# Strassen's seven products for the first feed-forward layer of a two-block decoder kernel, with its results kept in DRAM

## What is computed

```python
h = _rms(x, norm2_w[l]) * (1 + sc2) + sh2
x = x + g2 * (jnp.square(jax.nn.relu(h @ w_ff1[l])) @ w_ff2[l])
```

## Time and profile before

| | |
|---|---|
| median of three runs | 3284.92 us (3284.49 to 3287.08) |
| profiled execution: its own time | 3284.06 us |
| profiled execution: span, first to last instruction | 3282.3 us |
| PE busy | 3189.7 us, 97% |
| DVE, ACT, POOL busy | 45%, 26%, 35% |
| granted TensorE clock, mean | 0.993 |

### The profile page before, as it was taken

How to read it: one execution, slowest core, us unless ns; L and a number is a source line. 1 busy time by engine, 2 the same in 40 slices (tenths; PEclk the granted TensorE clock), 3 DMA queues, 4 the chain that set the end, 5 groups by cost and what they waited for, 6 DMA issues and landing times.

```text
span 3282.3 us, 39103 instructions
## 1 busy us (share of the span) xinstructions
PE 3189.7 (97%) x15278; PEld 2618.6 (80%) x15278; DVE 1463.8 (45%) x2213; ACT 863.1 (26%) x1410; POOL 1152.1 (35%) x880
## 2 busy tenths in 40 slices
PE   8999999998999899999999999999999999999999
PEld 5778888887787676788888888788788878888887
DVE  6765666566345775642222333336214731313131
ACT  4454445444222231400232233201101310101010
POOL 2332121221366321233222222353335753434342
PEclk9999999999999999999999999999999999999999
DMA  3321011100243221155123122421113321111112
GB/s 136 102 74 39 26 33 33 33 26 26 78 145 118 71 84 39 53 173 170 45 61 79 54 76 72 129 65 52 45 52 126 93 74 49 51 46 52 45 52 78
DMA packets 92208, 234.21 MB, mean 71 GB/s; under 512 B 7680, under 2 KB 33920, under 8 KB 91920
## 3 DMA queue, kind: packets, MB, share of 16 engines
q1 hardware_dynamic: 53504, 186.67, 18.4%
q10 hardware_dynamic: 38544, 45.24, 4.5%
HBM read 212.84 MB, written 19.04 MB: 71 GB/s over the span
## 4 chain that ended last, share of the span: by engine, by line
PE 91%; DVE 6%; ACT 2%; issue 1%; DMA 1%; ACTq 0%; SPq 0%; DVEq 0%
PE proj_bank L229 24%; PE proj_bank L231 23%; PE proj_bank L230 23%; PE aux_banks L229 3%; PE aux_banks L230 3%; PE aux_banks L231 3%; PE aux_banks L781 2%; PE aux_banks L862 2%; PE aux_banks L788 1%; PE aux_banks L1797 1%; PE aux_banks L2277 1%; PE aux_banks L563 1%; DVE aux_banks L1675 1%; PE aux_banks L2298 1%; DVE dil_k L2445 0%
## 5 line engine op out<-in xcount | busy, mean ns | idle before, releaser
L229 PE MATMUL proj_bank<-h_hi,slab_hi 128*128 128x512 f32 x2784 | 1102.9, 396 | 10.2 <-ACT y L629 2.8
L231 PE MATMUL proj_bank<-h_hi,slab_lo 128*128 128x512 f32 x2784 | 1086.0, 390 | 0.0
L230 PE MATMUL proj_bank<-h_lo,slab_hi 128*128 128x512 f32 x2784 | 1085.0, 390 | 0.0
L251 POOL CAST slab_hi<-slab_raw 128x1024 fp32r<-128x1024 f32 x290 | 308.8, 1065 | 2069.2 <-PE proj_bank L231 1554.4
L255 POOL TENSOR_TENSOR slab_lo<-slab_raw,slab_hi 128x512 fp32r<-128x512 f32 x580 | 836.5, 1463 | 23.2
L229 PEld LDWEIGHTS proj_bank<-h_hi,slab_hi 128*128 128x128 f32 x2784 | 523.7, 188 | 134.0 <-issue 17.8
L231 PEld LDWEIGHTS proj_bank<-h_hi,slab_lo 128*128 128x128 f32 x2784 | 523.1, 188 | 111.3
L230 PEld LDWEIGHTS proj_bank<-h_lo,slab_hi 128*128 128x128 f32 x2784 | 524.1, 188 | 106.4 <-issue 2.2
L229 PE MATMUL proj_bank<-ffn_hi,slab_hi 128*128 128x512 f32 x512 | 199.2, 389 | 0.4 <-issue 0.4
L230 PE MATMUL proj_bank<-ffn_lo,slab_hi 128*128 128x512 f32 x512 | 199.2, 389 | 0.0
L231 PE MATMUL proj_bank<-ffn_hi,slab_lo 128*128 128x512 f32 x512 | 199.2, 389 | 0.0
(11 more groups left out here) (407 smaller groups left out, 4076.1 us busy)
## 6 DMA issues: line engine op xcount, KB each, us to landing
slab_raw<-wts SPq DMA_DIRECT2D x292, 512.0 KB, 3.6
ada_w<-ada_w SPq DMA_DIRECT2D x40, 384.0 KB, 3.2
ada_w_early<-ada_w SPq DMA_DIRECT2D x24, 384.0 KB, 3.7
ssd_decay_rows<-decay_sums ACTq DMA_DIRECT2D x16, 512.0 KB, 4.2
dil_rows<-dilated_out ACTq DMA_DIRECT2D x12, 520.0 KB, 8.5
x_first<-xT SPq DMA_DIRECT2D x4, 1024.0 KB, 9.2
x<-xT ACTq DMA_DIRECT2D x4, 1024.0 KB, 6.5
x_kept<-x ACTq DMA_DIRECT2D x16, 256.0 KB, 3.1
```

The lines of the kernel that those rows point to most:

```text
L229: pe.matmul(bank, whi[:, slot, wk, :], hi[:, xk, cols], start=first and a == 0, stop=False)
L230: pe.matmul(bank, whi[:, slot, wk, :], lo[:, xk, cols], start=False, stop=False)
L231: mm = pe.matmul(bank, wlo[:, slot, wk, :], hi[:, xk, cols], start=False, stop=last and a == len(ks) - 1)
L251: pool.tensor_copy(whi[:, to], k.raw[:, slot]).then_inc(k.s_hi, 1)
```

## The change

The first quarter's first layer stays as it is. For quarters 1 to 3, two output tiles of 128 features are taken together as a pair (12 pairs). A pair is a 2 x 2 block problem: two halves of the contraction (4 tiles each), two output tiles, two token halves. It is computed by Strassen's scheme (the form with fewer additions) in seven products of 4 contraction tiles, 12 matmuls each, instead of eight.

- Weights: for each pair SP loads four 128x512 blocks (`A11`, `A12`, `a21`, `A22`) in three DMAs; POOL makes four sums (`S1` to `S4`), ACT makes the seven high parts (`pair_high`) and POOL the seven low parts. There are two sets of buffers, used by turns.
- Tokens: the combinations are made once, in the second half (`c` = 1) of the first quarter's first layer. For `j` = 0 to 3 DVE makes four sums of 128x512 into PSUM banks (`combined(j)`), ACT four high parts from them (`combined_high(j)`) and DVE four low parts (`combined_low(j)`).
- Products go to six PSUM banks by turns. ACT copies the first of a pair to SBUF; DVE adds the others (seven more additions, each with a bank and an SBUF tile) and squares four results.
- All squared results, the first quarter's too, go to DRAM (`fd`, 256 KB a store, from ACT's queue), and so does `x2` (`x2d`), whose place is used for the pairs' weights.
- The second layer runs afterwards in eighths of the contraction: 8 eighths x 8 slabs x 2 token halves, each 12 matmuls in one of the two old banks. Each eighth's input (2 MB) is loaded back and split by ACT (`eighth_high`) and DVE (`eighth_low`); weights come in half-slab doubles of 512 KB in a ring of three, split by POOL.

The core of the diff (of removed lines only those that are named in the text):

```diff
@@ mixer_out_stage @@
-    tmp = k.at("norm2_tmp", F + 104, [P, 4, HALF])
+    tmp = k.at("norm2_tmp", F, [P, KT, T])
@@ mixer_out_stage, block.tensor @@
-                pe.wait_ge(s_read, VISITS + n + 1)
+                if n < 2:
+                    pe.wait_ge(s_read, VISITS + n + 1)
+                else:
+                    pe.wait_ge(fp.s_squared, n - 1)
@@ mixer_out_stage, block.scalar @@
+        def ffn_store(c, f):
+            i = c * KT + f
+            act.wait_ge(fp.s_squared, i + 1)
+            act.dma_start(k.fd[f // KH, :, f % KH, cols_of(c)], fp.made[:, i % 4]).then_inc(k.s_x[i % 4], 16)
+        def combined_high(j):
+            act.wait_ge(fp.s_combined, 4 * j + 4)
+            for i in range(4):
+                act.activation(fp.thi[:, KH * (i // 2) + j, cols_of(i % 2)], fp.tsum(j, i), ACT.Copy).then_inc(fp.s_thi, 1)
         for f in range(KT):
             ffn_in(1, f)
+            ffn_store(f > 0, (f - 1) % KT)
+            if f < KH:
+                combined_high(f)
+            if f == KT - 2:
+                for i in range(4):
+                    pair_high(k, act, fp, 0, i)
@@ mixer_out_stage, block.vector @@
         def scaled(c, t):
-            if n >= 4:
-                dve.wait_ge(s_nlo, n - 3)
         def ffn_square(c, f):
+            dve.wait_ge(s_read, 2 + VISITS + i + 1)
+            dve.scalar_tensor_tensor(own, out_bank(i), 0.0, own, ALU.max, ALU.mult).then_inc(fp.s_squared, 1)
+        def combined(j):
+            t1, t2, t3, t4 = (fp.tsum(j, i) for i in range(4))
+            dve.tensor_tensor(t1, tmp[:, j, second], tmp[:, j, first], ALU.subtract).then_inc(fp.s_combined, 1)
+            dve.wait_ge(fp.s_combined, 4 * j + 1)
+            dve.scalar_tensor_tensor(t2, tmp[:, late, second], shift(late), t1, ALU.add, ALU.subtract).then_inc(fp.s_combined, 1)
+            dve.wait_ge(fp.s_combined, 4 * j + 2)
+            dve.scalar_tensor_tensor(t3, tmp[:, j, first], shift(j), t2, ALU.add, ALU.subtract).then_inc(fp.s_combined, 1)
+            dve.scalar_tensor_tensor(t4, tmp[:, late, first], shift(late), t2, ALU.add, ALU.subtract).then_inc(fp.s_combined, 1)
+        def combined_low(j):
+            for i in range(4):
+                dve.wait_ge(fp.s_thi, 4 * j + i + 1)
+                dve.tensor_tensor(fp.tlo[:, t, own], fp.tsum(j, i), fp.thi[:, t, own].bitcast(F32), ALU.subtract).then_inc(fp.s_tlo, 1)
         for f in range(KT):
             ffn_square(1, f)
+            if 1 <= f <= KH:
+                combined_low(f - 1)
+            if f < KH:
+                combined(f)
@@ ffn_stage, block.tensor @@
+        for p in range(FF_PAIRS):
+            for i, a in enumerate(PRODUCTS):
+                pe.wait_ge(k.s_split, N_WHOLE + N_PROD * p + i + 1)
+                if N_PROD * p + i >= BANKS:
+                    pe.wait_ge(*product_read(*divmod(N_PROD * p + i - BANKS, N_PROD)))
+                for j, (hi, lo) in enumerate(tokens(i)):
+                    pe.matmul(bank(p, i), n.hi(p, a)[:, j, :], hi, start=j == 0, stop=False)
+                    pe.matmul(bank(p, i), n.hi(p, a)[:, j, :], lo, start=False, stop=False)
+                    mm = pe.matmul(bank(p, i), n.lo(p, a)[:, j, :], hi, start=False, stop=j == KH - 1)
+                mm.then_inc(k.s_proj, 1)
+        for e in range(EIGHTHS):
+            for f in range(KT):
+                for c in range(2):
+                    pe.wait_ge(s_x2, 2 * i + c + 1)
+                    for j in range(KH):
+                        if f == 0 and c == 0:
+                            pe.wait_ge(s_flo, KH * e + j + 1)
...
@@ ffn_stage, block.scalar @@
+        for p in range(FF_PAIRS):
+            act.wait_ge(k.s_proj, product_done(p, 0))
+            act.activation(n.p1, bank(p, 0), ACT.Copy).then_inc(n.s_tensor, 1)
+            if p:
+                store(p - 1, 3)
+            if p < LAST:
+                for i in range(N_PROD):
+                    pair_high(k, act, n, p + 1, i)
+            if p == LAST:
+                eighth_high(0)
+            for which in range(3):
+                store(p, which)
@@ ffn_stage, block.vector @@
+            add(p, 1, n.u2, n.p1)
+            add(p, 2, n.u3, n.u2)
+            add(p, 3, n.made[:, 1], n.u3, 1)
+            add(p, 3, n.u2, n.u2)
+            square(1, at + 3)
+            add(p, 4, n.made[:, 2], n.u3, 2)
+            square(2, at + 5)
+            if p == LAST:
+                eighth_low(0, 0)
+                eighth_low(0, 1)
+            add(p, 5, n.made[:, 0], n.p1, 0)
+            square(0, at + 6)
+            if p == LAST:
+                eighth_low(0, 2)
+            add(p, 6, n.made[:, 3], n.u2, 3)
+            square(3, at + 7)
+        eighth_low(0, 3)
 @@ ffn_stage, block.gpsimd @@
+            def low(i):
+                a = PRODUCTS[i]
+                pool.wait_ge(k.s_hi, N_WHOLE + N_PROD * p + i + 1)
+                pool.tensor_tensor(n.lo(p, a), own(a), n.hi(p, a).bitcast(F32), ALU.subtract).then_inc(k.s_split, 1)
+            pool.wait_ge(n.s_loaded[p % 2], 48 * (p // 2 + 1))
+            if p >= 2:
+                pool.wait_ge(k.s_proj, product_done(p - 2, N_PROD - 1))
+            pool.tensor_tensor(own(S1), n.a21, own(A22), ALU.add).then_inc(n.s_sum, 1)
+            pool.wait_ge(n.s_sum, 4 * p + 1)
+            pool.tensor_tensor(own(S2), own(S1), own(A11), ALU.subtract).then_inc(n.s_sum, 1)
+            pool.tensor_tensor(own(S3), n.a21, own(A11), ALU.subtract).then_inc(n.s_sum, 1)
+            pool.wait_ge(n.s_sum, 4 * p + 3)
+            low(0)
+            pool.tensor_tensor(own(S4), own(A12), own(S2), ALU.subtract).then_inc(n.s_sum, 1)
+            pool.wait_ge(n.s_sum, 4 * p + 4)
+            for i in range(1, N_PROD):
+                low(i)
@@ ffn_stage, block.sync @@
+            else:
+                sp.wait_ge(k.s_proj, product_done(p - 2, 5))
+            sp.dma_start(n.first_two(p), wts[FP_0 + 2 * p].rearrange("p (a k) m -> p a k m", a=2)).then_inc(n.s_loaded[p % 2], 16)
...
+        sp.wait_ge(k.s_proj, product_done(LAST - 1, N_PROD - 1))
+        ring_load(0)
+        ring_load(1)
+        sp.wait_ge(k.s_proj, product_done(LAST, 0))
+        f_load(0)
+        x2_load(0)
+        ring_load(2)
+        sp.wait_ge(k.s_proj, product_done(LAST, 4))
+        f_load(1)
+        sp.wait_ge(k.s_proj, product_done(LAST, N_PROD - 1))
+        x2_load(1)
```

More of the change, by code:

```diff
@@ L2843, in _ @@
             squares(0, f)
+        keep(0)
         for f in range(KT):
@@ L2994, in _ @@
         pe.sem_inc(s_x2, 2)
[L2995 to L3004, removed]
+        for p in range(FF_PAIRS):
[3 more added lines that the diff above has]
+                    pe.wait_ge(*product_read(*divmod(N_PROD * p + i - BANKS, N_PROD)))
+                if p == 0 and i == 1:
+                    pe.wait_ge(n.s_tlo, 4 * KH)
+                for j, (hi, lo) in enumerate(tokens(i)):
[3 more added lines that the diff above has]
+                mm.then_inc(k.s_proj, 1)
@@ L3005, in _ @@
+        for e in range(EIGHTHS):
             for f in range(KT):
+                i, (d, half) = e * KT + f, divmod(e * KT + f, 2)
+                pe.wait_ge(k.s_split, SPLITS + i + 1)
                 for c in range(2):
[L3007 to L3025, removed]
+                    pe.wait_ge(s_x2, 2 * i + c + 1)
@@ new lines, in _ @@
+                    for j in range(KH):
+                        if f == 0 and c == 0:
+                            pe.wait_ge(s_flo, KH * e + j + 1)
+                        hi, lo = f_hi[e % 2][:, j, cols_of(c)], f_lo[e % 2][:, j, cols_of(c)]
+                        pe.matmul(k.bank[c][:], ring_hi[d % RING][:, half, j, :], hi, start=j == 0, stop=False)
+                        pe.matmul(k.bank[c][:], ring_hi[d % RING][:, half, j, :], lo, start=False, stop=False)
+                        mm = pe.matmul(k.bank[c][:], ring_lo[d % RING][:, half, j, :], hi, start=False, stop=j == KH - 1)
@@ L3048, in _, with add, square @@
     def _(dve):
-        def added(base):
+        def add(p, i, to, other, freed=None):
+            at = N_PROD * p
+            dve.wait_ge(k.s_proj, product_done(p, i))
+            if freed is not None:
+                dve.wait_ge(k.s_x[freed], n.stored + 16 * (4 + p))
+            return dve.tensor_tensor(to, bank(p, i), other, ALU.add).then_inc(n.s_added, 1)
+        def square(at, value):
+            own = n.made[:, at]
+            dve.wait_ge(n.s_added, value)
+            dve.scalar_tensor_tensor(own, own, 0.0, own, ALU.max, ALU.mult).then_inc(n.s_squared, 1)
@@ new lines, in kept, with f_load, x2_load, ring_load @@
+        def kept(e):
+            pairs = max(0, (KH * (e + 1) - KT) // 2)
+            for at in range(4):
+                sp.wait_ge(k.s_x[at], n.stored + 16 * (4 + pairs))
+        def f_load(e):
+            kept(e)
+            sp.dma_start(f_raw[e % 2][:], k.fd[e]).then_inc(s_fl[e % 2], 16)
+        def x2_load(b):
+            sp.wait_ge(s_moved, 32 + 16 * b)
```

(22 more changed lines are left out.)

256 lines of the change are left out of this document (168 added, 88 removed).

## The result

The changed kernel takes 3263.64 us (median of four, 3263.08 to 3265.84) against 3284.71 us before: ratio 0.9933, 95% interval 0.9920 to 0.9945, 21 us or 0.7% faster. The forecast was 3261.

What follows compares the result with a forecast made beforehand. PE was taken as the bound, without gaps in the feed-forward windows. From 3284.06, - 32.6 - 2.4 + 6.9 + 3.5 + 1.6 gave 3261.1; forecast 3261 us, own range 3254 to 3268, 8 in 10 for 3250 to 3276.

Steps and rivals of the forecast that it cites:

- 32.6 us for 144 matmuls: First layer, quarters 1 to 3: 1152 matmuls become 1008, so 144 at 0.2267 us each go, 32.6 us less.
- rival 4: Pairs: changing bank every 12 matmuls leaves PE at 1.2 GHz, 195 us more, 3456 us; 2 in 100.
- 2.4 us for the stop: First quarter's first layer, around the second token half's first group: PE's wait for DVE's low tokens goes, 2.4 us less.
- Token sums, 6.9 us: First quarter's second token half: a serial loop of 8.7 us against PE's 5.44 stalls groups 4, 5 and 6, 6.9 us.
- rival 2: Second token half: the token sums are hidden and their 6.9 us goes, 3254 us or a little under; 10 in 100.
- Pairs at no stall: Quarters 1 to 3, first layer: PE never waits, needing 19.04 us a pair against POOL's 17.1.
- The 12 us of lead: Pairs: POOL starts 1.8 us into the pair before, so its first low part is ready 12 us ahead of use.
- rival 1: Pairs: POOL becomes the bound at 24.8 us a pair, 57 us more, 3318 us; 5 in 100.
- The sign: Pairs: whether the change is faster or slower, said to be decided by POOL from about 22 us a pair.
- Eighth 0, 3.5 us: Start of the second layer: PE waits about 1.4 us for the third low part and 2.1 for the fourth.
- Half clock, 1.6 us: Second layer: one stretch at half speed, 3 us long, after a wait adds 1.6 us; in the token sums mostly hidden.

## Why the prediction held, step by step

- *32.6 us for 144 matmuls*: right, and now shown: 36 matmuls less are 8.2 us. The change of bank every 12 matmuls costs nothing (rival 4).
- *2.4 us for the stop*: right in kind; 2.2. What is left, 0.3 us, is PE still waiting for DVE's last low tokens.
- *Token sums, 6.9 us*: right in the mechanism and the groups (4, 5 and 6), so rival 2 fell; the size was 7.9 (the prediction's own terms give 6.8), and this is most of the 1.5 us by which the sum was off. ACT's copies in the changed kernel show the loop:

```profile
2635.20 0.63 ACT L2875 ACTIVATE ffn_made<-proj_bank 128x512 f32<-128x512 f32 x1
...
2643.76 0.63 ACT L2875 ACTIVATE ffn_made<-proj_bank 128x512 f32<-128x512 f32 x1
...
2652.80 0.63 ACT L2875 ACTIVATE ffn_made<-proj_bank 128x512 f32<-128x512 f32 x1
```

  8.6 and 9.0 us a turn, forecast 8.7. The first turn, from the copy at 2627.95 to the one at 2635.20, took 7.25 us, forecast 6.3. What I had too short is the first sum of a turn, which reads SBUF twice: I had put 0.7 us, and took the 1.77 of such an operation under POOL only for the upper bound. It took 0.69 in two of the four turns, 1.18 in one, and in the first

```profile
2629.19 1.81 DVE L3004 TENSOR_TENSOR aux_banks<-norm_tmp 128x512 f32<-128x512 f32 x1
```

- *Pairs at no stall*: right. POOL's work a pair is 15.1 us from the first sum to the last low part in the quiet case (2753.89 to 2768.97) and 15.9 at most, not 17.1. The 12 us of lead are 10: POOL starts a pair 3.4 us into the pair before and not 1.8, since SP's third load of a pair is issued 0.9 us after the first and lands 4.9 us later in the median. And they are there only from the third pair on. So rival 1 was priced too low: a POOL that is slow from the start pays nearly every microsecond over 19.04. The sign turns at about 21 us a pair, not 22: the kernel with four more sums, at 21.1, was 4 us slower than the kernel before.
- *Eighth 0, 3.5 us*: 3.6, for the reason given. That it fits so closely is in part luck. The prediction's own times give 3.4 us, and two of them missed in opposite ways: the first two low parts took 2.3 us and not 3.4, the third 2.2 and not 1.1 (2903.37 to 2905.59).
- *Half clock, 1.6 us*: right. There were two spells; the one in the token sums was hidden by the next late bank, as I had taken it, and the one at eighth 0 cost 1.9 us with the slower first steps. That it came was not certain: waits of 0.4 and 3.1 us at the same place, the same in sum, had none behind them in another run (below).

The largest open item is the end of the unchanged part. In thirteen profiles of the same code (eleven experiments, before and after) it lies between 2580.4 and 2584.2 us, and the spells of half clock ahead of it differ in number and length from run to run. Their total does not sort the runs: with 47.6 us at half clock ahead of it the moment lay at 2580.4 in one profile and at 2583.5 in another. The cause stays open.

## What to carry to other kernels

When side work is put into a stage that alternates two banks, add up the closed loop (copy, square, side work, and whatever the copying engine does in its program order before the next copy), not each engine's load: from 2627 to 2663 us ACT was busy for 11.3 of 36 us and DVE for 23.6, and PE waited. Leave light groups between the heavy ones, and put what the next stage waits for ahead of what nobody waits for; here this was worth 11 us more, half of what the seven products brought net. A lead of one engine over another has to be earned before it can be spent, so price a slower helper from its first round on.

## What the runs showed of the hardware that I had not expected

Two waits of the same length can have different prices. At eighth 0 PE waited 3.1 us in the kernel with the sums spread (2903.05 to 2906.37) and in the one with two more sums for POOL (2905.86 to 2909.18). Each came behind a wait of 0.4 us four microseconds before. Behind the first the matmuls were 0.43 us apart for eight steps (granted clock 0.50), behind the second they were at 0.23 after one step of 0.34 (granted clock 1.00). The changed kernel run again had the same pair of waits, and half clock behind it. So the length alone does not decide. Nor does a wait have to be long: in the changed kernel two waits at eighth 0, of 1.6 and 2.0 us with three matmuls between them, were followed by half clock from 2909.8 on (granted clock 0.51), 1.3 us after the second had ended, while the 12 waits of 1.5 to 2.2 us in the pairs of the kernel with four more sums, 21.1 us apart, had none behind them.
